# First head ranked in two steps, smaller first loads, and one weight chunk's second use moved behind the first gathers, in a decoder trunk on one core

## The chip, the cores and the metric

The kernel runs on one core of a Trainium2 chip. The metric is the device time of one execution in microseconds (us). The kernel before takes 1578.14 us (median of 3 runs, 1577.06 to 1578.72). Its profiled execution took 1575.86 us, with a span of 1574.0 us from the first to the last instruction.

## The reference

A trunk of two layers over 256 tokens with 1024 features, all in float32. Layer 0 mixes tokens with differential attention, layer 1 with a short gated convolution; behind each comes a product-key expert layer (PEER). Cut to what matters here:

```
def peer_ffn(h, w_q, sub_keys, u_tab, v_tab):
    q = (xt @ w_q).reshape(T, 8, 2, 128)
    s = einsum('thpd,hpkd->thpk', q, sub_keys)          # 2 x 128 scores per head
    s_top, i_top = lax.top_k(s, 16)
    cand = s_top[:, :, 0, :, None] + s_top[:, :, 1, None, :]          # 16 x 16 sums
    cand_idx = i_top[:, :, 0, :, None] * 128 + i_top[:, :, 1, None, :]
    best, pos = lax.top_k(cand, 16); idx = take_along_axis(cand_idx, pos)
    gates = softmax(best)
    act = einsum('chkd,cd->chk', u_tab[idx], x)          # 8 heads x 16 experts per token
    return einsum('chk,chkd->cd', gelu(act) * gates, v_tab[idx])

h = x
for i in range(2):
    h = h + (diff_attention if i == 0 else short_conv)(rmsnorm(h), ...)
    h = h + peer_ffn(rmsnorm(h), ...)
```

Each token picks 128 experts per layer, so the experts' rows (u and v side by side, 2048 floats) are fetched once per token and expert: 512 fetches of 128 rows, 1 MiB each.

## The kernel before

**Windows and slots.** The tokens are two blocks of 128. Window n = 0 and 1 are layer 0 on block 0 and 1, n = 2 and 3 layer 1 on the same blocks. A window's experts are 128 *slots*; slot s fetches one expert row per token. There are 512 slots in all. For each slot GpSimd (POOL) issues an indirect gather into one of the 8 places of `ring` (L643), VectorE (DVE) takes the dot product of the u half with the tokens (`dot`, L1239), ScalarE (ACT) makes gelu, weight and a diagonal matrix (`weigh`, L853 to L859), and TensorE (PE) adds the v half, scaled by that diagonal, into two accumulators (`add_expert`, L575). A gather for slot s waits until slot s-8 has been added (`v_used`). PE runs two slots behind in its own loop: at loop step s it does `add_expert(s-2)` and then the side work that is due at s.

**Weights.** All dense weights come as chunks of 1024 x 512 (2 MiB), issued by SyncE (SP) in the order of the list `loads` into 7 places: two in `wring` (0 and 1), four that lie over pairs of ring places (2 to 5), and `spare` (6). Before a chunk is loaded over another, SP waits in order until PE has finished the chunk that lay there (`written`). `(n, "in", c)` is input chunk c of window n, where c = 0, 1 are Q, 2, 3 are K, and 4, 5 are V; `(n, "out", c)` and `(n, "wq", c)` are the output and query chunks. Window 1's chunks 0, 4 and 5 are not loaded again: PE multiplies them from the places that window 0's copies still hold (`weights`, L297).

**Front.** Before the first slot each engine runs a straight list, `front()`: window 0's attention, its output projection, the query chunk wq 0 in two halves "a" and "b", the ranking of head 0 (`ranked`, L1037: two top-16 searches, the 16 x 16 sums, a top 16 of these, the indices), and window 1's chunks 0, 4 and 5 from places 4, 2 and 3. Since those places are ring places, the gathers of slots 0, 1 (place 4), 4, 5 (place 2) and 6, 7 (place 3) wait for these products (L630 to L638); slots 2 and 3 lie in place 5 and wait for `(0, "out", 0)`.

**Order in the slots.** What comes after is spread over the slots by tables: `AT[1]` for window 1's attention, `LATE_RANK_PROJECT` for wq 1 to 3 of window 0 (product at the slot given, ranking 13 slots later), `LATE_IN_PROJECT` for window 1's remaining input chunks (8 slots of product, then a copy, then on Q and K the norm `norm_qk`). Each of the 8 steps of a chunk's product is one contraction step k, recorded as two matmuls. The next lines are SP's order of loads and the tables:

```
later = [(1, "in", 2), (1, "in", 1), (0, "wq", 2), (1, "in", 3), (0, "wq", 3)]
loads += [(*what, (i + 1) % 2) for i, what in enumerate(later)]
LATE_RANK_PROJECT = {1: 0, 2: 25, 3: 41}
LATE_IN_PROJECT = {2: 9, 1: 17, 3: 33}
```

Of the kernel before, what the change touches and what calls it, by code (L numbers as in the profile page):

```python
# [14 lines left out]
P = 128  # L15
# [41 lines left out]
def steady_of(n):  # L57
# [7 lines left out]
    dict(q0=12, k0=22, q1=30, k1=46,  # L65
         logits0=24, bias0=25, max0=29, exp0=30, diff0=34, turn0=37, values0=40,
         logits1=48, bias1=49, max1=53, exp1=54, diff1=58, turn1=61, values1=64,
         norm0=45, norm1=66, y0=49, y1=70, out0=73, out1=81, h0=82, f0=83, h1=90, f1=91, scale=91,
         wq0=94, wq1=104, wq2=116, wq3=128),
# [54 lines left out]
def build(nc, consts, x_rows, x_cols, bias_rows, ffn_rows, w_qkv, w_o, conv_w_in, conv_w_out, peer_w_q, peer_keys, peer_uv, out):  # L124
    with ExitStack() as ctx:
# [80 lines left out]
        def pool_of(name, banks=None):  # L206
# [6 lines left out]
        x_cols_in = [sem("x_cols_in0"), sem("x_cols_in1")]  # L213
        const_in = sem("const_in")
# [4 lines left out]
        w_half_in = sem("w_half_in")  # L219
# [47 lines left out]
        loads += [(*what, (i + 1) % 2) for i, what in enumerate(later)]  # L267
# [6 lines left out]
        def ring_at(s):  # L274
            return (s + 4) % RING
# [43 lines left out]
        def _(pe):  # L319
# [22 lines left out]
            def project(pool, n, what, c, src, at):  # L342

                for k in range(KT):
                    yield at + k
                    project_part(pool, n, what, c, src, (k,))
# [29 lines left out]
            def mix_values(n, c):  # L376
                copied(pe, tt, *((n, "attn", 2 * c + kb) for kb in range(n + 1)))
                for m in range(n + 1):
                    copied(pe, ff if m else pp, (m, "in", 4 + c))
# [33 lines left out]
            def front():  # L413
# [3 lines left out]
                pe.wait_ge(w_half_in, 16)  # L417
# [3 lines left out]
                for k in every:  # L421
                    if k == 4:
                        pe.wait_ge(x_scaled, 2)
                        pe.wait_ge(w_in[4], 16)
# [58 lines left out]
                project_part(ff, 1, "in", 5, xT1, every)  # L483
# [35 lines left out]
            def output(n):  # L519
                at = steady_of(n)  # L520
                for c in range(2):
                    yield at[f"out{c}"]
                    if c == 0 and n == 1:
                        copied(pe, tt, (1, "y", 0), (1, "y", 1))
# [39 lines left out]
            def add_expert(s):  # L564

                n, k = divmod(s, SLOTS)
                if s == 0:
                    copied(pe, ff, (1, "in", 4), (1, "in", 5))
# [5 lines left out]
                for half in range(2):  # L574
                    mm = nc.tensor.matmul(acc[half][:, :], diag[:, s % RING, :], row[:, D + half * 512:D + (half + 1) * 512],  # L575
                                          start=(k == 0), stop=(k == SLOTS - 1))
                mm.then_inc(v_used, 1)

            front()
            sides = begun(late(1), late_input(2), turn_late("q", 0), late_input(1), turn_late("k", 0), attention(0), late(2),  # L580
                          turn_late("q", 1), late_input(3), late(3), turn_late("k", 1), turn_mixed(0), attention(1), turn_mixed(1),
                          output(1), turn_output(1), *(experts(1, c) for c in range(4)))
# [11 lines left out]
        def _(sp):  # L594
            def load(n, what, c):
                place, landed, _ = weights(n, what, c)
                matrix = {"in": in_dram[n // 2], "out": out_w_dram[n // 2], "wq": peer_w_q[n // 2]}[what]
                if (n, what, c) == (0, "in", 0):
                    half = KT * CHUNK // 2
                    sp.dma_start(place[:, 0:half], matrix[c][:, 0:half]).then_inc(w_half_in, 16)  # L600
                    sp.dma_start(place[:, half:], matrix[c][:, half:]).then_inc(landed, 16)
# [3 lines left out]
            sp.dma_start(xT[:, :, :].rearrange("p k t -> p (k t)"), x_cols[0]).then_inc(x_cols_in[0], 16)  # L605
            previous = {}
            for n, what, c, place in loads:
                if place in previous:
                    m, was, k = previous[place]
                    written(sp, pp, (m, "wqb" if (m, was, k) == (0, "wq", 0) else was, k))  # L610
# [5 lines left out]
            for b in range(2):  # L616
                for c in range(2):
# [6 lines left out]
        def _(pool):  # L624
            for n in range(WINDOWS):
                for k in range(SLOTS):
                    s = n * SLOTS + k
                    if k % TOPK == 0:
                        pool.wait_ge(idx_ready, s // TOPK + 1)
                    if s < RING:  # L630
                        if ring_at(s) < 2:
                            written(pool, ff, (1, "in", 4))
                        elif ring_at(s) < 4:
                            written(pool, ff, (1, "in", 5))
# [665 lines left out]
```

## Time and profile before

| | |
|---|---|
| median of 3 runs | 1578.14 us (1577.06 to 1578.72) |
| profiled execution | 1575.86 us, span 1574.0 us |
| PE, DVE, ACT, POOL busy | 1357.4, 1005.6, 594.8, 568.2 us |
| moved by DMA | 637.58 MB, mean 405 GB/s |
| granted TensorE clock, mean | 0.963 |

The page cuts the span into 40 slices of 39.35 us and gives for each the busy share of the engines and of the DMA engines and the GB/s moved. A busy share averages over stages with different limits, so it is read by stretches: the answers with windows give busy time, instructions, the granted clock, the DMA share and the GB/s of any stretch. The timeline gives single instructions with their start, their length and what ended the idle time before them.

### The profile page before, as it was taken

The page shows a single profiled execution, that of the slowest core. Times are in us where ns is not written, and L with a number is a line of the kernel's source. Part 1 is how long each engine was busy: PE and PEld are TensorE (multiplying, and loading weights), DVE is VectorE, ACT ScalarE, POOL GpSimd, SP SyncE. Part 2 cuts the span into 40 slices and gives each one's busy share as a digit, 9 for nine tenths or more (in the row PEclk, how much of TensorE's full clock was granted, in tenths as well). Part 3 has the DMA queues.
Part 4 walks back from the last instruction along what each step waited for, and adds up shares of the span by engine and source line. Part 5 has one row for each costly group of instructions (what it writes and reads, how often), then busy time and mean ns, then how long its engine had stood idle before and what let it go on. Part 6 is the DMA issues. An engine that isn't in the chain of part 4 may idle for free.

```text
span 1574.0 us, 13058 instructions
## 1 busy us (share of the span) xinstructions
PE 1357.4 (86%) x3288; PEld 587.2 (37%) x3288; DVE 1005.6 (64%) x2442; ACT 594.8 (38%) x1809; POOL 568.2 (36%) x516
## 2 busy tenths in 40 slices
PE   7899899888897988977989898879898887777777
PEld 3454344433343433333434343334343332222222
DVE  5686879964587864444467985444558896544454
ACT  1324354543342542332334443333334444333333
POOL 0024333543343433323444343323344453444341
PEclk9999999999998999989999899999899999999999
DMA  9469999999999999999999999999999999999996
GB/s 399 208 250 422 423 417 407 407 422 421 422 422 421 394 422 423 425 421 422 422 422 422 389 410 423 423 422 422 422 422 421 420 407 421 421 421 422 421 422 282
DMA packets 82297, 637.58 MB, mean 405 GB/s; under 512 B 9136, under 2 KB 9264, under 8 KB 10544
## 3 DMA queue, kind: packets, MB, share of 16 engines
q0 software_dynamic: 73728, 536.90, 82.4%
q1 hardware_dynamic: 7200, 93.85, 14.3%
q10 hardware_dynamic: 1296, 6.00, 0.9%
q8 instruction: 28, 0.46, 0.1%
q14 instruction: 45, 0.37, 0.1%
HBM read 635.67 MB, written 1.05 MB: 405 GB/s over the span
## 4 chain that ended last, share of the span: by engine, by line
DMA 39%; PE 36%; DVE 16%; ACT 4%; issue 4%; DVEq 0%; POOL 0%; SPq 0%; POOLq 0%; ACTq 0%
DMA ring<-in_peer_uv_dram,idx 38%; PE acc L575 22%; PE pp L338 10%; DVE ring L1239 7%; PE acc L338 1%; ACT diag L859 1%; PE tt L351 1%; DVE top_i L1025 1%; ACT weight L855 1%; DVE top L1021 1%; ACT L853 1%; ACT L722 1%; DVE row_f L1070 1%; ACT gelu L853 1%; PE pp L425 1%
## 5 line engine op out<-in xcount | busy, mean ns | idle before, releaser
L575 PE MATMUL acc<-ring,diag 128*128 128x512 f32 x2048 | 1003.9, 618 | 160.4 <-ACT diag L859 150.9
L1239 DVE CUSTOM_DVE_ANT_0 ring<-ring,xf 128x1024 f32<-128x1024 f32 x512 | 626.9, 1226 | 492.2 <-DMA ring<-in_peer_uv_dram,idx 480.5
L643 POOL DMA_INDIRECT ring<-in_peer_uv_dram,idx x512 | 568.0, 1109 | 982.9 <-PE acc L575 856.2
L575 PEld LDWEIGHTS acc<-ring,diag 128*128 128x128 f32 x2048 | 382.8, 196 | 705.3 <-issue 692.8
L853 ACT ACTIVATE gelu<-dots 128x1 f32<-128x1 f32 x512 | 103.5, 202 | 836.7 <-DVE dots L1239 836.4
L859 ACT ACTIVATE diag<-const,weight 128x128 f32<-128x128 f32 x512 | 205.5, 401 | 16.8
L855 ACT ACTIVATE weight<-gelu,gates 128x1 f32<-128x1 f32 x512 | 150.8, 295 | 16.6
L338 PE MATMUL pp<-wring,xT 128*128 128x512 f32 (+1 forms) x272 | 130.5, 578 | 1.2 <-ACT xT L662 1.2
L338 PE MATMUL pp<-wring,rows 128*128 128x512 f32 x192 | 99.6, 600 | 0.0
L338 PEld LDWEIGHTS pp<-wring,xT 128*128 128x128 f32 x272 | 52.0, 194 | 59.4 <-issue 56.5
L338 PE MATMUL pp<-wring,qTa 128*128 128x512 f32 x112 | 57.4, 601 | 0.0
L338 PEld LDWEIGHTS pp<-wring,rows 128*128 128x128 f32 x192 | 36.8, 193 | 45.8 <-issue 45.8
L1239 DVE DVE_READ_ACCUMULATOR2_ANT dots<- 128x1 f32 x512 | 41.9, 82 | 0.0
L410 PE MATMUL ss<-keysT,qT 128*128 128x128 f32 x128 | 21.0, 315 | 20.6 <-issue 20.6
L351 PE MATMUL tt<-const,rows 128*128 128x128 f32 x144 | 23.1, 285 | 17.0 <-DVEq L1199 11.3
L1025 DVE FIND_INDEX8 top_i<-top,score 128x8 uint32<-128x128 f32 x128 | 34.2, 285 | 0.0
L351 PEld LDWEIGHTS tt<-const,rows 128*128 128x128 f32 x144 | 17.7, 146 | 39.8 <-DVEq L1199 14.6
L338 PEld LDWEIGHTS pp<-wring,qTa 128*128 128x128 f32 x112 | 21.7, 195 | 27.2 <-issue 27.2
L410 PEld LDWEIGHTS ss<-keysT,qT 128*128 128x128 f32 x128 | 19.6, 224 | 30.6 <-issue 30.5
L1021 DVE MAX8 top<-score 128x8 f32<-128x128 f32 x128 | 28.1, 280 | 3.4 <-ACT score L718 2.4
L1025 DVE FIND_INDEX8 pos<-best,pick 128x8 uint32<-128x256 f32 x64 | 26.1, 418 | 0.0
L338 PE MATMUL pp<-wring,xf 128*128 128x512 f32 x48 | 25.0, 602 | 0.0
(114 smaller groups left out, 636.5 us busy)
## 6 DMA issues: line engine op xcount, KB each, us to landing
wring<-in_peer_w_q_dram SPq DMA_DIRECT2D x14, 2048.0 KB, 11.9
wring<-in_conv_w_in_dram SPq DMA_DIRECT2D x12, 2048.0 KB, 12.0
wring<-in_w_qkv_dram SPq DMA_DIRECT2D x5, 2048.0 KB, 12.0
ring<-in_peer_uv_dram,idx POOLq DMA_INDIRECT x512, 15.3
wring<-in_conv_w_out_dram SPq DMA_DIRECT2D x4, 2048.0 KB, 11.7
ring<-in_w_qkv_dram SPq DMA_DIRECT2D x3, 2048.0 KB, 32.0
wring<-in_w_o_dram SPq DMA_DIRECT2D x3, 2048.0 KB, 12.6
ring<-in_w_qkv_dram SPq DMA_DIRECT2D x2, 1024.0 KB, 8.6
```

Source lines behind the costliest of these rows:

```text
L338: mm = nc.tensor.matmul(bank[:, 0:width], src[:, k, :], by_row[:, k, columns], start=(k == 0), stop=(k == KT - 1))
L351: t = nc.tensor.transpose(bank[:, j * P:(j + 1) * P], tile, ident)
L410: mm = nc.tensor.matmul(bank[:, j * P:(j + 1) * P], qT[:, j, :], keysT[:, 4 * c + j, :], start=True, stop=True)
L425: mm = nc.tensor.matmul(bank[:, :], xT[:, k, :], by_row[:, k, :], start=(k == 0), stop=(k == KT - 1))
L575: mm = nc.tensor.matmul(acc[half][:, :], diag[:, s % RING, :], row[:, D + half * 512:D + (half + 1) * 512], start=(k == 0), stop=(k == SLO ...
L643: nc.gpsimd.indirect_dma_start(dst, None, uv_dram, bass.IndirectOffsetOnAxis(idx[:, at:at + 1], 0)).then_inc(landed, 16)
L853: nc.scalar.activation(gelu[:, r:r + 1], dots[:, r:r + 1], ACT.Gelu_apprx_tanh).then_inc(gelu_done, 1)
L855: nc.scalar.activation(weight[:, r:r + 1], gelu[:, r:r + 1], ACT.Copy, scale=gates[:, at:at + 1]).then_inc(weight_ready, 1)
L859: nc.scalar.activation(diag[:, r, :], ident, ACT.Copy, scale=weight[:, r:r + 1]).then_inc(diag_ready, 1)
L1021: ins = nc.vector.max(t, v)
L1025: ins = nc.vector.max_index(i, t, v)
L1239: nc.vector.tensor_tensor_reduce(row[:, 0:D], row[:, 0:D], xf[:, s // SLOTS % 2, :], 1.0, 0.0, ALU.mult, ALU.add, dots[:, s % RING:s % RIN ...
```

## The change

Six edits, all but the last in the front and in the first 90 slots.

1. *First loads.* Block 0's columns come in two halves (k 0 to 3, 4 to 7), the first weight chunk in a quarter, a quarter and a half; DVE scales the first half as soon as it is there, PE starts with the first quarter. ACT issues the load of block 0's rows behind the second quarter.
2. *First head.* `first_head` replaces `ranked` for head 0: it finds the best 8 of each half, ranks their 8 x 8 sums, writes 8 indices and releases the gathers of slots 0 to 7; then it does the rest (16 x 16 sums without the 8 found). Block 1's `scale_for_mixer` goes ahead of `add_output`, and the norm of window 1's chunk 0 out of the front into slots 8 to 10.
3. *Chunk (1, "in", 5)* (V of tokens 128 to 255) leaves the front and is multiplied in slots 8 to 15. Chunk (0, "in", 5) therefore lies in `wring` place 0, (0, "in", 1) and (0, "out", 1) in place 3, and both wq 0 and wq 1 in place 1.
4. *Ring.* Slots 0 to 7 now take ring places 6, 7, 2, 3, 4, 5, 0, 1: the first four wait for window 0's output chunks, the next two for (1, "in", 0), the last two for (1, "in", 4).
5. *Tables.* Window 1's other chunks, its attention and window 0's wq 2 and 3 shift by up to 8 slots, and wq 2 is loaded ahead of (1, "in", 1).
6. *End.* The last slot's first half signals by itself; DVE adds it to h while the second half is multiplied, and ACT stores the last quarter of the output.

On SP the chunks from window 0's output on stand so before; in brackets is what the issue waits for, here that PE has finished the chunk that lay there:

```order
L603 DMA ring<-in_w_o_dram 128x4096 [waits pp_written1]
L603 DMA wring<-in_w_o_dram 128x4096 [waits pp_written0]
L603 DMA wring<-in_peer_w_q_dram 128x4096 [waits pp_written1] x2
L603 DMA wring<-in_w_qkv_dram 128x4096 [waits pp_written1]
L603 DMA wring<-in_w_qkv_dram 128x4096 [waits pp_written0]
L603 DMA wring<-in_peer_w_q_dram 128x4096 [waits pp_written1]
```

And so now:

```order
L610 DMA ring<-in_w_o_dram 128x4096 [waits pp_written1]
L610 DMA ring<-in_w_o_dram 128x4096 [waits pp_written0]
L610 DMA wring<-in_peer_w_q_dram 128x4096 [waits pp_written1] x2
L610 DMA wring<-in_w_qkv_dram 128x4096 [waits pp_written1]
L610 DMA wring<-in_peer_w_q_dram 128x4096 [waits pp_written0]
L610 DMA wring<-in_w_qkv_dram 128x4096 [waits pp_written0]
```

The pair of `in_peer_w_q` rows is wq 0 and wq 1. Before, wq 1 waited for (0, "out", 1), now for wq 0's half "b"; the next row, (1, "in", 2), waited for that half "b" and now waits for (1, "in", 5), with wq 2 behind it.

On PE, the end of the front and the first slot before (`acc<-ring,xf` are window 1's chunks from ring places, `uv_in` the landing of a gather):

```order
L338 MATMUL acc<-ring,xf 128x512 [waits ff_read1,w_in2]
L338 MATMUL acc<-ring,xf 128x512 x7
L338 MATMUL acc<-ring,xf 128x512 [waits ff_read0,w_in3]
L338 MATMUL acc<-ring,xf 128x512 x7
L338 MATMUL pp<-wring,xT 128x512 [waits pp_read0,w_in0]
L338 MATMUL pp<-wring,xT 128x512
L575 MATMUL acc<-ring,diag 128x512 [waits uv_in4,diag_ready,ff_read0,ff_read1]
```

And now:

```order
L341 MATMUL acc<-ring,xf 128x512 [waits ff_read1,w_in2]
L341 MATMUL acc<-ring,xf 128x512 x7
L341 MATMUL pp<-wring,xT 128x512 [waits pp_read0,w_in1]
L341 MATMUL pp<-wring,xT 128x512
L581 MATMUL acc<-ring,diag 128x512 [waits uv_in6,diag_ready,ff_read1,ff_read0]
```

The 8 steps of (1, "in", 5) are gone from between (1, "in", 4) and the first slot.

On PE at loop steps 15 to 17 now, where (1, "in", 5) ends and (1, "in", 2) begins:

```order
L341 MATMUL pp<-wring,xf 128x512
L581 MATMUL acc<-ring,diag 128x512 [waits diag_ready,uv_in0]
L581 MATMUL acc<-ring,diag 128x512
L341 MATMUL pp<-wring,xf 128x512 [waits pp_read0,w_in0]
L581 MATMUL acc<-ring,diag 128x512 [waits diag_ready,uv_in1]
```

The row with `w_in0` is the first step of (1, "in", 2); its weights can only be issued once the product in the first row is done.

The diff, cut to its core:

```
-    dict(q0=12, k0=22, q1=30, k1=46,
-         logits0=24, bias0=25, max0=29, exp0=30, diff0=34, turn0=37, values0=40,
...
+    dict(q0=12, k0=29, q1=45, k1=53,
+         logits0=31, bias0=32, max0=36, exp0=37, diff0=41, turn0=44, values0=47,
...
-LATE_RANK_PROJECT = {1: 0, 2: 25, 3: 41}
+LATE_RANK_PROJECT = {1: 0, 2: 24, 3: 48}
-LATE_IN_PROJECT = {2: 9, 1: 17, 3: 33}
+LATE_IN_PROJECT = {5: 8, 2: 16, 1: 32, 3: 40}
+FIRST_NORM = 8
...
-        first = [("in", 0, 4), ("in", 2, 5), ("in", 1, 0), ("in", 3, 1), ("in", 4, 2), ("in", 5, 3), ("out", 0, 5),
-                 ("out", 1, 0), ("wq", 0, 1), ("wq", 1, 0)]
+        first = [("in", 0, 4), ("in", 2, 5), ("in", 1, 3), ("in", 3, 1), ("in", 4, 2), ("in", 5, 0), ("out", 0, 5),
+                 ("out", 1, 3), ("wq", 0, 1), ("wq", 1, 1)]
-        later = [(1, "in", 2), (1, "in", 1), (0, "wq", 2), (1, "in", 3), (0, "wq", 3)]
+        later = [(1, "in", 2), (0, "wq", 2), (1, "in", 1), (1, "in", 3), (0, "wq", 3)]
-        loads += [(*what, (i + 1) % 2) for i, what in enumerate(later)]
+        loads += [(*what, i % 2) for i, what in enumerate(later)]
...
-            return (s + 4) % RING
+            return (6, 7, 2, 3, 4, 5, 0, 1)[s % RING]
...
-                project_part(ff, 1, "in", 5, xT1, every)
...
+            sp.dma_start(xT[:, 0:4, :].rearrange("p k t -> p (k t)"), x_cols[0][:, 0:4 * P]).then_inc(x_first_in, 16)
+            sp.dma_start(first_place[:, 0:CHUNK * 2], in_dram[0][0][:, 0:CHUNK * 2]).then_inc(w_first_in[0], 16)
+            sp.dma_start(xT[:, 4:KT, :].rearrange("p k t -> p (k t)"), x_cols[0][:, 4 * P:]).then_inc(x_cols_in[0], 16)
...
+            def first_head():
+                half = TOPK // 2
+                copied(dve, ss, (0, "scorea", 0))
+                rows2 = [score[:, 0, j, :] for j in range(2)]
+                whole(top8(rows2, [top[:, k, 0:half] for k in range(2)], [top_i[:, k, 0:half] for k in range(2)]))
+                link(nc.vector.tensor_copy(top_f[:, 0:2, 0:half], top_i[:, 0:2, 0:half]))
+                few = pick[:, 48:52, :].rearrange("p a c -> p (a c)")
...
+                whole(top8([few], [best[:, 0, 0:half]], [pos[:, 0, 0:half]]))
+                first_indices(0, half, 3)
+                for j in range(2):
+                    ins = nc.vector.match_replace(rows2[j], top[:, j, 0:half], rows2[j], LOW)
+                link(ins)
...
+                first_indices(half, TOPK, 4)
+                link(nc.vector.tensor_tensor(best_e[:, 0, :], best[:, 0, :], best[:, 0, 0:1].to_broadcast([P, TOPK]), ALU.subtract))
...
-                whole(ranked(0, 0, "a", range(0, 1)))
+                first_head()
                 gate_values(0, 0, range(0, 1))
-                whole(norm_qk(ff, 1, 0))
...
                 for c in range(2):
+                    if n == WINDOWS - 1 and c == 1:
+                        dve.wait_ge(v_used, ALL)
```

## Rows read from the trace of the kernel before

**Rows 1.** The page: GB/s in 40 slices of 39.35 us, and the bytes.

```profile
GB/s 399 208 250 422 423 417 407 407 422 421 422 422 421 394 422 423 425 421 422 422 422 422 389 410 423 423 422 422 422 422 421 420 407 421 421 421 422 421 422 282
DMA packets 82297, 637.58 MB, mean 405 GB/s; under 512 B 9136, under 2 KB 9264, under 8 KB 10544
```

**Rows 2.** Windows: length, busy PE, PEld, DVE, ACT, POOL, clock, DMA share, GB/s.

```profile
58.50:82.40 23.90, 19.16 (x57) 9.30 (x58) 10.22 (x35) 4.55 (x11) 0.00 (x0) 0.93 0.01 2
82.00:112.00 30.00, 28.77 (x95) 16.55 (x95) 25.35 (x93) 5.21 (x13) 6.40 (x6) 1.00 0.67 241
107.00:226.00 119.00, 108.16 (x278) 48.31 (x277) 88.45 (x227) 52.90 (x151) 44.45 (x39) 0.97 1.01 420
226.00:329.00 103.00, 90.25 (x263) 43.30 (x262) 94.37 (x261) 51.57 (x147) 43.27 (x37) 0.95 1.00 408
```

**Rows 3.** Timeline: SP's issues of wq 1 and (1, "in", 2).

```profile
82.41 0.33 SPq L603 DMA_DIRECT2D wring<-in_peer_w_q_dram  x1
93.64 0.33 SPq L603 DMA_DIRECT2D wring<-in_w_qkv_dram  x1
```

**Rows 4.** Timeline: POOL's gathers of slots 0 and 6.

```profile
101.55 1.07 POOL L643 DMA_INDIRECT ring<-in_peer_uv_dram,idx  x1 [101.10 <-DVEq L1078]
113.43 0.94 POOL L643 DMA_INDIRECT ring<-in_peer_uv_dram,idx  x1 [3.96 <-PE acc L338]
```

**Rows 5.** Line L603, SP's weight chunks of 2 MiB: issue to landing.

```profile
DMA to landing us min/median/max: 7.7/12.0/37.7
```

**Rows 6.** Timeline: the first chunks on PE, ACT's next load, the K norm.

```profile
8.81 8.62 PE L425 MATMUL pp<-ring,xT 128*128 128x512 f32 x16 [8.81 <-DMA ring<-in_w_qkv_dram]
16.23 0.34 ACTq L728 DMA_DIRECT2D spare<-in_bias_rows_dram  x1
17.26 7.03 PE L338 MATMUL pp<-ring,xT 128*128 128x512 f32 x16
30.00 0.69 DVE L943 TENSOR_TENSOR rows<-rows,root 128x512 f32<-128x512 f32 x1
30.99 1.04 PE L351 MATMUL tt<-const,rows 128*128 128x128 f32 x8
```

**Rows 7.** Timeline: DVE and ACT around the ranking of head 0.

```profile
78.55 0.69 DVE L1004 TENSOR_TENSOR h<-h,pp 128x512 f32<-128x512 f32 x1 [5.61 <-PE pp L338]
88.35 1.23 DVE L899 CUSTOM_DVE_ANT_0 scratch<-h 128x1024 f32<-128x1024 f32 x1 [0.19 <-DVE xf L1015]
90.19 0.38 ACT L718 ACTIVATE score<-ss 128x256 f32<-128x256 f32 x1 [0.92 <-PE ss L410]
91.83 0.49 DVE L1021 MAX8 top<-score 128x8 f32<-128x128 f32 x2
98.66 0.69 DVE L1064 TENSOR_TENSOR pick<-pos_f,const 128x512 f32<-128x512 f32 x1
102.48 0.69 DVE L904 TENSOR_TENSOR scratch<-rows 128x512 f32<-128x512 f32 x1
107.44 1.23 DVE L1239 CUSTOM_DVE_ANT_0 ring<-ring,xf 128x1024 f32<-128x1024 f32 x1 [0.19 <-DVE rows L943]
```

**Rows 8.** Timeline: PE's additions of slots 0 to 2.

```profile
116.37 1.96 PE L575 MATMUL acc<-ring,diag 128*128 128x512 f32 x4 [1.49 <-ACT diag L859]
119.02 1.88 PE L575 MATMUL acc<-ring,diag 128*128 128x512 f32 x4
121.59 1.88 PE L575 MATMUL acc<-ring,diag 128*128 128x512 f32 x4
```

**Rows 9.** Waits (us, times, longest): PE in 160 to 226 us, DVE in 220 to 230.

```profile
PE acc L575 <- ACT diag L859: 9.1, 4, 3.6
...
DVE ring L1239 <- DMA ring<-in_peer_uv_dram,idx: 5.7, 2, 4.4
```

**Rows 10.** Timeline: the end.

```profile
1570.03 1.52 DVE L1231 TENSOR_TENSOR h<-h,acc 128x512 f32<-128x512 f32 x2 [3.13 <-PE acc L575]
1570.80 1.17 SPq L619 DMA_DIRECT2D out_dram<-h  x2
```

More of the change, by code:

```diff
@@ L345, in project @@
                     yield at + k
+                    if (n, what, c, k) == (1, "out", 0, 4):
+                        copied(pe, tt, (1, "y", 1))
                     project_part(pool, n, what, c, src, (k,))
@@ L576, in add_expert @@
                                           start=(k == 0), stop=(k == SLOTS - 1))
+                    if s == ALL - 1 and half == 0:
+                        mm.then_inc(v_first_used, 1)
                 mm.then_inc(v_used, 1)
             front()
[L580 to L582 removed]
+            sides = begun(late(1), late_input(5), turn_late("q", 0), late_input(2), late(2), turn_late("k", 0), attention(0),
+                          late_input(1), turn_late("q", 1), late_input(3), late(3), turn_late("k", 1), turn_mixed(0), attention(1),
+                          turn_mixed(1), output(1), turn_output(1), *(experts(1, c) for c in range(4)))
             for n in (2, 3):
@@ L616, in _ @@
             for b in range(2):
-                for c in range(2):
+                for c in range(2 - b):
                     sp.wait_ge(h_finished, 2 * (2 + b) + c + 1)
@@ L633, in _ @@
                         elif ring_at(s) < 4:
[L634 removed]
+                            written(pool, pp, (0, "out", 1))
                         elif ring_at(s) < 6:
@@ new lines, in first_indices @@
+            def first_indices(first, last, bits):
+                span = 1 << bits
+                count = last - first
+                where = pos[:, 0, first:last]
+                link(nc.vector.tensor_scalar(pos2[:, 0, 0, 0:count], where, bits, None, ALU.logical_shift_right))
+                link(nc.vector.tensor_scalar(pos2[:, 0, 1, 0:count], where, span - 1, None, ALU.bitwise_and))
+                link(nc.vector.tensor_copy(pos_f[:, 0, :, 0:count], pos2[:, 0, :, 0:count]))
+                shape = [P, 2, count, span]
+                hot = pick[:, 32:48, 0:span].rearrange("p (h k) a -> p h k a", h=2)
+                link(nc.vector.tensor_tensor(hot, pos_f[:, 0, :, 0:count].unsqueeze(3).to_broadcast(shape),
+                                             iota[:, 0:span].unsqueeze(1).unsqueeze(1).to_broadcast(shape), ALU.is_equal))
+                link(nc.vector.tensor_tensor(hot, hot, top_f[:, 0:2, 0:span].unsqueeze(2).to_broadcast(shape), ALU.mult))
+                link(nc.vector.tensor_reduce(row_f[:, 0, :, 0:count], hot, AX.X, ALU.add))
+                link(nc.vector.scalar_tensor_tensor(out=idx_f[:, 0, 0:count], in0=row_f[:, 0, 0, 0:count], scalar=float(NKEYS),
+                                                    in1=row_f[:, 0, 1, 0:count], op0=ALU.mult, op1=ALU.add))
+                link(nc.vector.tensor_copy(idx[:, first:last], idx_f[:, 0, 0:count]))
+                dve.sem_inc(idx_ready, 1)
```

74 lines of the change are left out of this document (52 added, 22 removed).

## The prediction

> **What bounds the kernel now.** I first read the page's GB/s line: outside the first three slices and the last one it stands at 389 to 425, mostly at 421 or 422, and 637.58 MB are moved in all [rows 1]. At 422 GB/s these bytes alone take 1511 us of the span of 1574.0. So the DMA engines are the bound, and no byte goes away: the same 512 gathers, the same chunks. The change can gain only where the DMA engines are idle or underfed, 63 us in all. To find these places I took windows, and grouped them into stretches [rows 2]. From 58.5 to 82.4 us nothing moves (2 GB/s): the chunks of the front have landed and no place is free. From 82 to 112 us it is 241 GB/s, that is 7.23 MB. From 107 to 226 us it is 420, full. From 226 to 329 us it is 408, so 3.4 us are lost against 422 (103 x 14/422), with DVE busy for 94.37 of 103 us. What is lost later lies at the borders of windows, which the change leaves as they are, and at the end.
>
> **How I book.** Where the DMA engines are full before and behind a change, the end shifts by the difference in bytes moved up to a common point, divided by 0.422 MB/us.
>
> **First loads.** PE starts at 8.81 us, when the first half chunk lands, and works 8.62 us, so it could start and end up to 3 us sooner. But the next chunk, (0, "in", 2), is there only at 16.23: ACT's issue at that time had waited for it, and the bytes ahead of it are the same. PE took it up behind its first chunk, at 17.4, and so gains 1.2 us at most [rows 6]. The K norm on DVE hangs on ACT's copies, which come behind that same landing, and still ends at 30.69 (30.00 + 0.69). PE's turns of Q and K ran from 30.99 to 32.03; now the turn of Q runs earlier, that of K from about 30.8 to 31.35. The rest of the front is then 0.7 us earlier. Ends: 0 and 1.2; I take 0.7.
>
> The DMA engines work at 399 GB/s in the first slice already [rows 1]. The Trainium skill, "Perfetto Trace Analysis", section "DMA Optimizations", says that splitting transfers may help if the DMA engines are generally idle, which they are not here. By that rule this term would be 0 and the forecast 0.7 us later; I hold against it that PE waits for one landing, not for all bytes.
>
> **First head.** Block 1's mixer scale (88.35 to 91.7 us, 3.4 us) moves into DVE's idle 5.61 us ahead of the addition at 78.55 [rows 7], which hide it; uncovered it would cost its 3.4. The ranking then starts with the score, which ACT has at 90.6 (90.19 + 0.38), minus 0.7: at 89.9 instead of 91.83. Its steps up to the first 8 indices are shorter forms of rows 7's: two MAX8 (0.49) and two searches for their indices (as long), with gaps 1.2 us; the 64 sums and their best 8 about 0.9; small index steps and casts at 0.17 to 0.2 each, six of them, 1.2; three passes over 128 elements where one over 512 takes 0.69, about 0.8. That is 4.1 us, so the first gather goes at 94.1 instead of 101.55 [rows 4]. The second half takes as long as the rest of the old ranking and a little more, about 6.5 us, the gates 1; at 101.6 the first dot can follow. Before it came at 107.44, behind a norm of 5.0 us (from 102.48) that now lies in slots 8 to 10.
>
> **What the early gathers replace.** Four, then six gathers can be issued from 94.1 to about 101, two more when PE ends (1, "in", 4) at 105.2; before, the last two places came free at 113.43 [rows 4]. But SP pays for it. wq 1 was issued at 82.41, (1, "in", 2) at 93.64 [rows 3]. Now wq 1 waits for what released the latter and goes at 92.9, and (1, "in", 2) only near slot 15. So the idle stretch lasts to 93 and not to 82.4, and a chunk of 2.1 MB, 5.0 us, no longer fills it. From there on the engines are full: wq 1 and six gathers of 1.05 MB are 8.4 MB, 20 us of work, and the next two come after 12. By 112 us: a chunk alone took 7.7 us to land [rows 5] and 5.0 us are its bytes, so 1.6 us go by until the full rate (an estimate), and 17.5 us at 0.42 are 7.36 MB, against 7.23 before. That is 0.13 MB, 0.3 us gained. With the front's shift at 0 or 1.2 instead of 0.7 it runs from 0.4 lost to 0.8 gained. I take 0.3: seven microseconds of earlier indices pay mostly for the chunk that left the gap.
>
> **(1, "in", 5) out of the front.** A chunk's 8 steps take PE 6.9 us (7.03 by the modelled ends [rows 6]), so PE reaches slot 0 at 113.4 - 6.9 - 0.7 = 105.8, and with the same 3 us for ACT's copy and first diagonal the first addition comes at about 109 instead of 116.37. A slot with one step takes PE 2.57 us (119.02 to 121.59) [rows 8]. Loop step 15 ends at 109 + 13 x 2.57 + 1.7, near 144. Until then no chunk is loaded, gathers take 2.48 us each and 4 or 5 are outstanding: full.
>
> **The new wait at slot 16.** At 144 us SP issues (1, "in", 2), and PE asks for it one slot later. Beside gathers a chunk lands in 12.0 us [rows 5], so PE stands for 10 us, to about 156. Behind it wait the additions from slot 15 on, the copies of that chunk on ACT and, through the ring, the gathers from slot 23 on. The cover: outstanding at 144 are 5 gathers, (1, "in", 2) and wq 2, together 9.4 MB or 22 us of DMA work, so the engines do not run dry in these 10 us. At 156 both kernels have added 15 slots, and PE still owes 7 steps of a chunk, 6 us. Before, PE waited for 9.1 us on diagonals between 160 and 226 us [rows 9]; it owes less than it idled. So the wait costs 0, and if this cover fails, up to 6 us.
>
> **Attention and ranking in the slots.** From slot 38 (at 222 us, where DVE last waits for gathers [rows 9]) to slot 75 (329 us) DVE is the bound. The new tables put one more norm (5.0 us) and one more difference (2.5) into slots 39 to 74 and take some 3 us of ranking out: 4.5 us more. But one chunk less has been loaded by slot 38, so this slot comes 5.0 us earlier. Slot 75 then comes at 328.9 - 0.3 - 5.0 + 4.5 = 328.1, which beside the 0.3 is 0.5 us gained. Ends: 3.4 gained (nothing underfed any more) and 4.5 lost (the added work without the earlier start).
>
> **End.** Behind the last matmuls come two additions (1570.03, 1.52 us) and two stores, issued by 1571.97, and the span ends at 1574.0 [rows 10]. Now the first addition runs beside the second half's matmuls (0.94, half of rows 8's 1.88), the second follows them, and the last store is issued about 0.76 us sooner. Ends 0 and 1; I take 0.75.
>
> **Sum.** 0.3 + 0 + 0.5 + 0.75 = 1.55 us. The profiled execution took 1575.86 and would take 1574.3. It lies 2.3 us under the median of the runs shown; taking that as an offset that stays, the forecast is 1578.14 - 1.55 = 1576.6 us. A measurement of this kernel can tell about 0.2%, 3.2 us, from no change, so the forecast is: no measurable change.
>
> **Rivals.**
> - *The underfed stretch fills up* (faster, 0.28). For it: slot 38 comes 5 us earlier, and the first norm falls into slots in which DVE has idle time, since the engines are full and the gathers late there. Against: more of DVE's work than before now lies in slots 39 to 74. Price: 3.4 in place of 0.5, with 0.8 in the front and 0.75 at the end 5 us, 1573.2. It decides from 418 GB/s in the stretch from 226 to 329 us.
> - *The wait at slot 16 is passed on* (slower, 0.16). Place: PE at loop step 16. If the chunk lands late, or PE's idle 9.1 us lay where they can't take up what it owes, 6 us arrive at slot 38 with the DMA engines dry: 1578.1 + 6 - 1.1 = 1583. It decides from a landing more than 22 us behind the issue, or a DMA share under 0.95 between 150 and 226 us.
> - *The early gathers bring their whole lead of 7 us* (0.02): 1570.4, if the engines were idle there anyway. Rows 3 speak against it: wq 1 fills just these microseconds.
>
> **Chances.** Forecast 0.54, with its own range 1574.5 to 1579.5; the two faster cases together 0.30; slower 0.16. For 8 in 10 the range runs from the first rival, 1573.0, to where two thirds of the second are paid, 1581.5. Faster by over 0.2% 0.30, within 0.2% 0.54, slower 0.16.
>
> **What would show it.** First gather near 94, first addition near 109; SP's wq 1 at 93 and nothing moved from 58.5 to 93; a PE wait of 8 to 12 us near 145 with a DMA share of 1.0 beside it; slot 38 near 218 and slot 75 near 328 us; 0.75 us less between the last matmul and the end. Wrong would be: a first gather after 98 us, a DMA share under 0.95 anywhere from 95 to 226 us, or the stretch from 226 to 329 us under 400 or over 418 GB/s.

## The result, and the profile after

The changed kernel takes 1585.65 us (median of 6 runs, 1584.09 to 1588.75), the kernel before on the same chip 1576.69 us (6 runs, 1574.19 to 1578.72): the ratio is 1.0061 with a 95% interval of 1.0046 to 1.0076. It is 9.0 us slower, outside the range given, while the forecast was no measurable change. The profiled execution after took 1588.75 us with a span of 1586.9 us, 12.9 us longer than the span before. It lies 3.1 us above its median and the one before 0.8 us below its own, so the account in bytes below is of this pair of executions (12.9 us) and not of the medians (9.0 us). Of the kernel before on the chip of e9 to e11, one execution of 29 took 1594.18 us at a mean granted clock of 0.847, which widens the intervals of those three runs.

The page of the changed kernel, GB/s in slices (39.67 us each) and the bytes:

```profile
GB/s 396 205 184 423 421 425 313 418 420 423 424 420 422 390 422 424 421 423 424 421 422 423 400 401 424 420 422 422 422 422 421 421 405 421 422 420 422 421 422 297
DMA packets 82586, 637.58 MB, mean 402 GB/s; under 512 B 9169, under 2 KB 9297, under 8 KB 10961
```

The bytes are the same as in [rows 1]. Two slices stand out: the third (184 instead of 250) and the seventh (313 instead of 407). All the others differ by 15 GB/s at most, some up and some down. So there are two places of loss, and they can be priced by bytes. Windows of the changed kernel (length, busy PE, PEld, DVE, ACT, POOL, clock, DMA share, GB/s), against [rows 2]:

```profile
58.50:100.10 41.60, 35.41 (x120) 20.18 (x120) 25.37 (x89) 10.44 (x33) 0.00 (x0) 0.92 0.01 3
82.00:112.00 30.00, 28.77 (x98) 16.60 (x98) 19.95 (x80) 5.66 (x16) 5.92 (x6) 1.00 0.37 144
107.00:226.00 119.00, 107.75 (x281) 49.27 (x280) 84.81 (x221) 46.28 (x130) 39.91 (x39) 0.96 1.01 422
226.00:350.00 124.00, 104.61 (x293) 49.21 (x292) 103.18 (x287) 58.05 (x170) 47.12 (x40) 0.93 0.94 386
260.00:270.00 10.00, 8.23 (x16) 3.97 (x17) 5.36 (x13) 7.71 (x18) 0.93 (x1) 0.66 0.21 82
```

The kernel before in the last two of these windows:

```profile
226.00:350.00 124.00, 111.25 (x312) 52.61 (x311) 106.04 (x279) 59.57 (x173) 55.08 (x46) 0.96 1.00 411
260.00:270.00 10.00, 8.46 (x34) 4.21 (x34) 9.17 (x21) 7.69 (x18) 3.33 (x3) 1.00 1.02 425
```

From 82 to 112 us 4.32 MB were moved instead of 7.23, and 2.91 MB at 0.422 MB/us are **6.9 us**. From 107 to 226 us nothing is lost (422 against 420). From 226 to 350 us it is 25 GB/s less for 124 us, 3.10 MB or **7.3 us**. The end gives 0.8 us back (below). The sum, 13.4 us, stands against 12.9 us of span.

**The first loss starts at 8 us.** Timeline of the changed kernel (start, length, what ended the idle time), against [rows 6]:

```profile
6.22 9.87 PE L432 MATMUL pp<-ring,xT 128*128 128x512 f32 x16 [6.22 <-DMA ring<-in_w_qkv_dram]
8.02 0.34 ACTq L743 DMA_DIRECT2D h<-in_x_rows_dram  x1
18.89 1.23 DVE L917 CUSTOM_DVE_ANT_0 scratch<-h 128x1024 f32<-128x1024 f32 x1 [11.43 <-DMA h<-in_x_rows_dram]
24.06 0.20 ACT L751 ACTIVATE lam_s<-lam_s 128x2 f32<-128x2 f32 x1 [4.11 <-DVEq L944]
24.17 1.25 ACT L672 ACTIVATE rows<-pp,scale_mix 128x512 f32<-128x512 f32 x2
34.24 0.69 DVE L961 TENSOR_TENSOR rows<-rows,root 128x512 f32<-128x512 f32 x1
```

PE does start earlier, 6.22 instead of 8.81. But ACT issues the load of block 0's rows (512 KB) only at 8.02, behind the wait for the second quarter. SP has by then queued its chunks one behind the other, and the rows are in use 10.9 us after their issue. DVE computes the mixer's scale from them and, right behind it, the small sums `lam_sum`. ACT stands for these sums (`DVEq L944`), and its copies need the scale (line L672, `scale_mix`). They begin at 24.17 instead of 19.93, 4.24 us late. DVE's norms of Q and K follow one behind the other, and the K norm ends at 34.93 instead of 30.69 us, again 4.24 late. Before, the load was issued at 1.19 us and DVE read the rows at 9.16:

```profile
1.19 0.45 ACTq L726 DMA_DIRECT2D h<-in_x_rows_dram  x1
9.16 1.22 DVE L899 CUSTOM_DVE_ANT_0 scratch<-h 128x1024 f32<-128x1024 f32 x1 [2.45 <-DMA h<-in_x_rows_dram]
19.93 0.67 ACT L656 ACTIVATE rows<-pp,scale_mix 128x512 f32<-128x512 f32 x1
```

PE, idle for part of that time, shows a granted clock of 0.83 from 30 to 40 us, where before it had 1.00, and 0.83 from 60 to 80 us (0.91 before). 1.00 is 2.4 GHz throughout; 0.83 is a mean of the two levels, 2.4 and 1.2 GHz, over the stretch:

```profile
30.00:40.00 10.00, 7.48 (x21) 3.20 (x19) 8.64 (x33) 1.95 (x3) 0.00 (x0) 0.83 1.00 420
60.00:80.00 20.00, 15.82 (x42) 7.37 (x41) 11.72 (x45) 5.64 (x20) 0.00 (x0) 0.83 0.00 0
```

The score is ready at 97.04 us, 6.5 later than before: 4.24 us are the K norm's, and 2.2 were added on the way. Such an addition also differs between executions with the same front. e3 below has the front of the change, and its K norm ends at 34.74; from 30 to 40 us it shows 1.00, and its score is ready at 95.11, 1.9 us earlier than here. PE's wait ahead is the same in both, 2.52 us for the K norm, but the six matmuls that follow its turn take 4.44 us here and 2.74 in e3. e8 below has the front of the kernel before, with the K norm at 30.73; from 60 to 80 us it shows 0.83, and its score is ready at 92.47, 1.9 us later than before. In order:

```profile
30.00:40.00 10.00, 7.49 (x30) 3.73 (x29) 8.61 (x33) 1.95 (x3) 0.00 (x0) 1.00 1.02 429
60.00:80.00 20.00, 15.99 (x44) 7.96 (x45) 8.91 (x31) 2.69 (x5) 0.00 (x0) 0.83 0.00 0
```

The dip from 30 to 40 us is in two of the four profiled executions with late rows (after and e5, but not e2 and e3) and in none of the nine with early rows; the one from 60 to 80 us comes with either. So about 2 of the 6.5 us came with a clock that a late load didn't bring every time. In bytes: e3 moves 170 GB/s from 82 to 112 us, 5.0 us less than the kernel before, where this execution lacks 6.9. Timeline around the ranking of the changed kernel:

```profile
96.66 0.38 ACT L734 ACTIVATE score<-ss 128x256 f32<-128x256 f32 x1 [0.92 <-PE ss L415]
100.11 0.33 SPq L610 DMA_DIRECT2D wring<-in_peer_w_q_dram  x1
101.12 0.17 DVE L1147 CAST idx<-idx_f 128x8 uint32<-128x8 f32 x1
101.63 1.07 POOL L659 DMA_INDIRECT ring<-in_peer_uv_dram,idx  x1 [101.18 <-DVEq L1148]
```

The shorter ranking works: 4.6 us from score to gather instead of 11.0. It only makes good the delay. The first gather starts as in [rows 4]. But wq 1, issued at 82.41 before [rows 3], goes only at 100.11, and so the DMA engines stand still from 58.5 to 100 us. The chunk that left this gap is missed in full.

**The wait at slot 16 came, and cost nothing.** Changed kernel, SP's next issues and PE:

```profile
153.86 1.88 PE L581 MATMUL acc<-ring,diag 128*128 128x512 f32 x4
154.06 0.33 SPq L610 DMA_DIRECT2D wring<-in_w_qkv_dram  x1
154.43 0.43 SPq L610 DMA_DIRECT2D wring<-in_peer_w_q_dram  x1
165.50 2.07 PE L341 MATMUL pp<-wring,xf 128*128 128x512 f32 x2 [9.76 <-DMA wring<-in_w_qkv_dram]
```

PE stood for 9.76 us, from 155.7 to 165.5, while the engines moved 426 GB/s.

**The second loss is in slots 41 to 50.** Timeline of DVE, PE and POOL there:

```profile
243.67 1.22 DVE L1314 CUSTOM_DVE_ANT_0 ring<-ring,xf 128x1024 f32<-128x1024 f32 x1
251.04 1.22 DVE L1314 CUSTOM_DVE_ANT_0 ring<-ring,xf 128x1024 f32<-128x1024 f32 x1
253.41 3.05 PE L581 MATMUL acc<-ring,diag 128*128 128x512 f32 x4 [4.12 <-ACT diag L875]
255.58 1.23 DVE L1314 CUSTOM_DVE_ANT_0 ring<-ring,xf 128x1024 f32<-128x1024 f32 x1 [0.18 <-DVE rows L961]
256.25 1.06 PE L356 MATMUL tt<-const,scratch 128*128 128x128 f32 x4
261.77 1.09 PE L356 MATMUL tt<-const,rows 128*128 128x128 f32 x4 [4.46 <-ACT scratch L672]
268.22 0.93 POOL L659 DMA_INDIRECT ring<-in_peer_uv_dram,idx  x1 [10.56 <-PE acc L581]
```

Three consecutive dots (slots 42 to 44) are 7.4 and 4.5 us apart, where the engines' pace is one gather in 2.48 us. Between them DVE works off the ranking of wq 2, the norm of (1, "in", 1) and the attention's difference, which the new tables place in the same slots. PE waits 4.12 us for a diagonal. Then it waits a second time, at loop step 45. The pool `tt` has two banks. The turns of the attention at steps 44 and 45 hold both, and the turn of Q (`q1=45`) needs the first of them back; ACT frees it only behind the `weigh` of slot 45, which itself waits for that slot's dot. This costs 4.46 us more. POOL, held by `v_used`, stands for 7.53 us ahead of its gather at 256.73 and for 10.56 us ahead of the one at 268.22, and between 260 and 270 us the DMA engines run at a share of 0.21, 82 GB/s.

**The end.** Changed kernel, against [rows 10]:

```profile
1581.73 1.96 PE L581 MATMUL acc<-ring,diag 128*128 128x512 f32 x4 [0.52 <-ACT diag L875]
1582.86 0.69 DVE L1306 TENSOR_TENSOR h<-h,acc 128x512 f32<-128x512 f32 x1 [2.28 <-PE acc L581]
1583.64 0.33 SPq L631 DMA_DIRECT2D out_dram<-h  x1
1583.72 0.69 DVE L1306 TENSOR_TENSOR h<-h,acc 128x512 f32<-128x512 f32 x1 [0.17 <-PE acc L581]
1584.50 0.35 ACTq L887 DMA_DIRECT2D out_dram<-h  x1
```

From the start of the last four matmuls to the end of the span it is 5.2 us (1581.73 to 1586.9); before it was 6.0 us:

```profile
1568.04 1.96 PE L575 MATMUL acc<-ring,diag 128*128 128x512 f32 x4 [0.52 <-ACT diag L859]
```

### The profile page after: what moved, and what is told of

The parts are those of the page before. It is cut to its first block, busy times and chain, and to the rows that moved or that the text cites. A ratio compares the mean times of both kernels' runs of the same rounds, so it can differ in the third digit from the quotient of the medians.

```text
span 1586.9 us, 13075 instructions
## 1 busy us (share of the span) xinstructions
PE 1363.1 (86%) x3288; PEld 587.2 (37%) x3288; DVE 1006.1 (63%) x2452; ACT 595.2 (38%) x1809; POOL 563.6 (36%) x516
## 4 chain that ended last, share of the span: by engine, by line
DMA 42%; PE 36%; DVE 14%; issue 4%; ACT 4%; POOL 0%; DVEq 0%; SPq 0%; POOLq 0%; ACTq 0%
DMA ring<-in_peer_uv_dram,idx 40%; PE acc L581 23%; PE pp L341 10%; DVE ring L1314 6%; PE tt L356 1%; PE acc L341 1%; ACT diag L875 1%; ACT weight L871 1%; DMA wring<-in_w_qkv_dram 1%; DVE top_i L1043 1%; DMA h<-in_x_rows_dram 1%; DVE top L1039 1%; PE ss L415 1%; ACT gelu L869 1%; DVE pick L1085 1%
## 5 line engine op out<-in xcount | busy, mean ns | idle before, releaser
L341 PE MATMUL pp<-wring,qTa 128*128 128x512 f32 x96 | 49.0, 592 | 0.0
L341 PE MATMUL pp<-wring,xf 128*128 128x512 f32 x64 | 34.8, 626 | 9.8 <-DMA wring<-in_w_qkv_dram 9.8
L1043 DVE FIND_INDEX8 top_i<-top,score 128x8 uint32<-128x128 f32 x128 | 34.2, 285 | 0.0
L415 PE MATMUL ss<-keysT,qT 128*128 128x128 f32 x128 | 19.3, 297 | 13.4 <-issue 13.4
L341 PEld LDWEIGHTS pp<-wring,qTa 128*128 128x128 f32 x96 | 18.5, 193 | 23.2 <-issue 23.2
L1043 DVE FIND_INDEX8 pos<-best,pick 128x8 uint32<-128x256 f32 (+1 forms) x64 | 25.8, 415 | 0.0
```

The lines of the kernel that those rows point to most:

```text
L341: mm = nc.tensor.matmul(bank[:, 0:width], src[:, k, :], by_row[:, k, columns], start=(k == 0), stop=(k == KT - 1))
L415: mm = nc.tensor.matmul(bank[:, j * P:(j + 1) * P], qT[:, j, :], keysT[:, 4 * c + j, :], start=True, stop=True)
L1043: ins = nc.vector.max_index(i, t, v)
```

## The experiments

The theory after the result: loss A comes from the late issue of block 0's rows, loss B from what the tables stack in slots 41 to 50. The rivals: A comes from the four split transfers or from the displaced wq 1, and B follows from A or from the wait at slot 16. Each ratio is to the kernel before on the same chip. The unaltered change did not run beside e1 to e4.

**e1: the rows issued at once.** The change, without ACT's wait:

```
-                act.wait_ge(w_first_in[1], 16)
                 act.dma_start(h[:, 0, :], x_rows[0]).then_inc(x_in[0], 16)
```

> The changed kernel, but block 0's rows are loaded right behind the constants, as before the change. Theory H (the late load of these rows delays DVE's first statistics, ACT's first copy and with it the whole front): rows land near 9 us, first gather near 94 to 95 us instead of 101.6, and the end is 6 to 8 us earlier than the changed kernel's, 1578 to 1580 us. Rival (the front is held by PE or by the first chunks, the rows' load only lies beside it): first gather still after 100 us, time within 2 us of the changed kernel's 1585.7.

Measured: 1582.34 us, ratio 1.0043 [1.003, 1.0057]. Windows of e1:

```profile
82.00:112.00 30.00, 27.28 (x92) 15.63 (x91) 22.20 (x85) 9.04 (x24) 7.88 (x8) 1.00 0.55 222
226.00:350.00 124.00, 103.97 (x294) 49.25 (x294) 102.05 (x270) 57.29 (x164) 44.86 (x40) 0.93 0.95 390
```

The first gather goes at 96.11 us and the front moves 222 GB/s instead of 144, which is 5.5 us by bytes. The median of e1 falls by 3.3 us against the change's first runs and by 5.6 against its later ones (e5), less than the 6 to 8 expected. Counted over the kernel before on each chip it is 2.4 and 5.0 us, and the interval overlaps that of the change, so the time of e1 alone is a weak witness; the bytes and e4 carry the finding. Loss B stays (390 GB/s), so it does not follow from A.

**e2: the rows issued late, in the kernel before.** The counter-test:

```
+                act.wait_ge(w_half_in, 16)
                 act.dma_start(h[:, 0, :], x_rows[0]).then_inc(x_in[0], 16)
```

> The kernel before, but ACT waits for the first half weight chunk before it issues the load of block 0's rows. Theory H: rows land near 19 us instead of 9, first gather 5 to 8 us later than 101.6, time 5 to 8 us over the kernel before (1582 to 1585 us). Rival (the late load alone costs nothing; it costs only with the other edits of the front): same as before within 1.5 us.

Measured: 1581.0 us, ratio 1.0029 [1.002, 1.0038], 5.3 us over the kernel before, at the low end of the 5 to 8 expected. Timeline of e2:

```profile
7.29 0.34 ACTq L727 DMA_DIRECT2D h<-in_x_rows_dram  x1
18.12 1.23 DVE L900 CUSTOM_DVE_ANT_0 scratch<-h 128x1024 f32<-128x1024 f32 x1 [11.68 <-DMA h<-in_x_rows_dram]
105.89 1.08 POOL L643 DMA_INDIRECT ring<-in_peer_uv_dram,idx  x1 [105.44 <-DVEq L1079]
```

One wait on one load, with nothing else of the change, gives the same landing (10.8 us), the K norm at 34.2 (33.47 + 0.69, not shown) and 4.3 us on the first gather. From 82 to 112 us e2 moves 188 GB/s instead of 241, 3.8 us by bytes. Loss A is shown from both sides: taking the wait out moves the front forward, and putting it in alone moves it back.

**e3: the second Q turn out of step 45.** The change with

```
-    dict(q0=12, k0=29, q1=45, k1=53,
+    dict(q0=12, k0=29, q1=48, k1=53,
```

> The changed kernel with one number of the table altered: PE turns window 1's second Q chunk at slot 48 instead of 45, where two turns of the attention weights already stand. Theory T (three turns at one loop step need a bank that ACT frees only behind a later slot's dot product, so PE stops for it and the gathers dry up): no PE wait on the copy of the attention weights near 260 us, the 10 us with 82 GB/s go, 3 to 6 us faster than the changed kernel. Rival D (DVE has three jobs stacked in slots 41 to 43, and that alone starves the ring): PE waits for diagonals instead, under 1.5 us gained.

Measured: 1583.0 us, ratio 1.0047 [1.0033, 1.0061]; the wait on `ACT scratch` is gone. Windows of e3:

```profile
226.00:350.00 124.00, 108.03 (x305) 50.69 (x304) 106.41 (x285) 61.70 (x178) 45.02 (x41) 0.96 0.99 405
260.00:270.00 10.00, 7.22 (x33) 4.20 (x32) 6.48 (x12) 7.96 (x19) 1.88 (x2) 1.00 0.81 279
```

405 instead of 386 GB/s is 5.6 us by bytes; the median is 2.7 to 5.0 us lower (1.7 and 4.4 counted over the kernel before on each chip; this interval too overlaps that of the change). So by bytes most of loss B hung on one turn that asked for a bank still held.

**e4: both mended** (e1 and e3 together).

> The changed kernel with both edits: block 0's rows loaded early, second Q turn at slot 48. If the two losses are separate places in the ledger of bytes, the gains add: 9 to 14 us under the changed kernel, 1572 to 1577 us. If the second loss only takes up room that the first one left (or the reverse), the sum is smaller by several microseconds.

Measured: 1578.59 us, ratio 1.0018 [1.0009, 1.0027]. Windows of e4:

```profile
82.00:112.00 30.00, 27.28 (x92) 15.61 (x91) 23.30 (x91) 9.08 (x23) 8.02 (x9) 1.00 0.60 240
226.00:350.00 124.00, 108.68 (x306) 51.12 (x307) 105.45 (x273) 60.36 (x173) 43.87 (x41) 0.96 0.99 405
```

First gather at 94.79, wq 1 at 93.28, 7.20 MB from 82 to 112 us, first addition at 109.14: the front of the prediction (94.1, 92.9, 7.36 MB, 109), once the rows come in time. e1 has the same front and moved 222 GB/s there where e4 moved 240; the 1.3 us between them is what single executions differ by. The two repairs together give 7.1 us against the change's first runs and 9.4 against e5, where the single ones add up to 6.0 and 10.6. The interval is clear of that of the change. wq 1 is displaced in e4 as in the change, so this rival for loss A is out. The 1572 to 1577 us expected were missed by 1.6 us. What is left is 405 against 411 GB/s; e6 asks whether that is DVE's stack.

**e5: the change once more**, on the chip of e6 to e8.

> The changed kernel once more, unaltered, beside the next ones on the same chip: about 1585 us and 9 us over the kernel before. First gather between 99 and 102 us. If it comes out under 1583, part of the 3.3 and 2.7 us read from the two single edits was between chips and not theirs.

Measured: 1587.99 us, ratio 1.0066 [1.0052, 1.008]. The result stands.

**e6: the attention's steps apart.** e4, and the difference, its turns and its values three slots later, the value norm and its turn two slots later, the Q turn ahead of them:

```
-    dict(q0=12, k0=29, q1=48, k1=53,
-         ... diff0=41, turn0=44, values0=47, ... norm0=52, ... y0=56, ...
+    dict(q0=12, k0=29, q1=46, k1=53,
+         ... diff0=44, turn0=47, values0=50, ... norm0=54, ... y0=58, ...
```

> The changed kernel with early row load, and window 1's first attention half pulled apart on DVE: difference, turns and values 3 slots later (44, 47, 50), its value norm at 54, the second Q turn at slot 46 ahead of the turns. Theory D2 (what is left of the loss in the stretch from 226 to 350 us is DVE's stack of ranking, norm and difference in slots 41 to 43): no DVE slot over 6 us there, the stretch at 410 GB/s or more where e4 had 405, 1 to 2 us under e4's 1578.6. Rival (the stretch is bound by DVE's total work, so spreading it does nothing): 405 GB/s and e4's time within 0.8 us.

Measured: 1575.59 us, ratio 0.9994 [0.9985, 1.0003]. Windows of e6:

```profile
82.00:112.00 30.00, 27.28 (x91) 15.56 (x90) 23.25 (x91) 9.09 (x23) 8.19 (x9) 1.00 0.60 242
226.00:350.00 124.00, 110.42 (x313) 51.86 (x314) 107.16 (x276) 61.08 (x177) 48.75 (x42) 0.97 1.01 417
```

Same work, no less of it on DVE (107.16 us busy, more than in any other of these windows), and yet 417 GB/s. It was not the amount but the place. It is 3.0 us quicker than e4 on another chip, with intervals that don't overlap, more than the 1 to 2 expected; the bytes say 3.5. The wait at slot 16 is still in it, so loss B doesn't come from there. With all three repairs the change is what was forecast, no measurable difference.

**e7: the first head alone.** The kernel before, with `first_head` in place of `ranked`, the two scales moved ahead, and a ring order in which four early gathers find a place:

```
-            return (s + 4) % RING
+            return (6, 7, 4, 5, 0, 1, 2, 3)[s % RING]
...
-                whole(ranked(0, 0, "a", range(0, 1)))
+                first_head()
```

> The kernel before with the two-step ranking of head 0, block 1's mixer scale moved ahead, and the ring order 6, 7, 4, 5, 0, 1, 2, 3, but with all weight chunks, products, first loads and tables as before. Ledger theory (early gathers pay in full when the weight chunks keep their place in the gap): first gather near 95 us, the DMA engines busy from 95 us on without the hole near 101 us, about 9.2 MB moved from 82 to 112 us instead of 7.2, 3 to 5 us faster than before. Rival (DVE's later stretch takes the gain back): under 1 us gained.

Measured: 1575.1 us, ratio 0.9989 [0.998, 0.9998]. Windows of e7:

```profile
82.00:112.00 30.00, 28.77 (x96) 16.48 (x95) 24.10 (x96) 5.22 (x13) 6.81 (x6) 1.00 0.79 309
112.00:226.00 114.00, 104.94 (x277) 47.78 (x276) 85.80 (x223) 54.79 (x155) 41.08 (x38) 0.97 1.01 411
```

Here wq 1 and (1, "in", 2) stay in the gap and the early gathers come on top: 9.27 MB by 112 us against 7.23, worth 4.8 us. But from 112 to 226 us 11 GB/s less are moved, which takes 3.0 us back. The net is 1.2 us in the medians, less than the 3 to 5 expected. The trace shows where the second stretch falls off, in its first 20 us (423 GB/s before), and what the next gather waits for:

```profile
112.00:132.00 20.00, 18.51 (x44) 7.94 (x43) 16.56 (x43) 12.53 (x33) 8.25 (x8) 1.00 0.98 358
118.81 0.94 POOL L647 DMA_INDIRECT ring<-in_peer_uv_dram,idx  x1 [3.41 <-PE acc L575]
```

The ring has 8 places, so the ninth gather waits for the first addition. That addition comes at 116.08 against 116.37 before, since the additions still stand behind the same products of the front, and the ninth gather goes at 118.81 against 118.59. So the eight gathers use up their lead, and no further gather can follow earlier than before. No run tests this by itself, but e9 and e11 show the same dip (362 and 359 GB/s).

**e8: the end alone.** The kernel before with only edit 6.

> The kernel before with only the split of the last slot and its stores. 0.75 us less between the last matmul and the end; in the time 0.3 to 1 us less, hardly to be told from nothing.

Measured: 1575.25 us, ratio 0.9997 [0.9988, 1.0006]: no difference that the runs can tell. In the profile of e8 it is 5.1 us from the last matmuls (1570.26) to the end of the span (1575.4), 0.8 less than before.

**e9: first head and end.** e7 with the new end.

> The kernel before with two parts of the change: the first head in two steps (with its ring order and the block 1 scale moved ahead) and the new end. Each alone measured 0.9989 and 0.9997 of the kernel before. Theory (the changed parts are additive, both are small gains): the profile shows about 0.8 us less from the last matmul to the end (5.1 to 5.2 instead of 5.96), a first gather at 94 to 96, and a time 1.0 to 2.5 us under the kernel before, ratio 0.9984 to 0.9993. Rival (the first head's gain lies inside what executions differ by, and only the end is real): 0.9993 to 1.0000.

Measured: 1573.15 us, ratio 0.9976 [0.9955, 0.9996], 3.3 us under the kernel before on that chip (1576.46), more than the 1.0 to 2.5 expected.

**e10: the split loads alone**, in the kernel before, the rows issued at once:

```
+            sp.dma_start(xT[:, 0:4, :] ..., x_cols[0][:, 0:4 * P]).then_inc(x_first_in, 16)
+            sp.dma_start(first_place[:, 0:CHUNK * 2], ...).then_inc(w_first_in[0], 16)
+            sp.dma_start(xT[:, 4:KT, :] ..., x_cols[0][:, 4 * P:]).then_inc(x_cols_in[0], 16)
```

> The kernel before with the first loads split as in the change (columns in halves, first chunk in a quarter, a quarter and a half), but ACT issues block 0's rows at once, as before. Theory A (the split is harmless, the loss of the change sits in the late issue of the rows alone): DVE reads the rows at 9 to 10 us, the K norm ends within 1.5 us of 30.7, ratio 0.9990 to 1.0005, first gather 100 to 102.5. Theory B (four transfers beside the rows slow the rows down, so the split itself costs): rows land at 12 us or later, K norm past 32, first gather past 103, ratio 1.001 to 1.003. The prediction's own term was 0.7 us earlier.

Measured: 1575.96 us, ratio 0.9991 [0.997, 1.0011]. DVE reads the rows at 8.70 us and the first gather goes at 101.06, 0.5 earlier than before. The K norm ends at 30.95. The split is harmless, and the rival that it slows the rows down is out. Whether the split gains its half microsecond the time can't tell.

**e11: first head, end and split together.**

> First head in two steps, new end and the split first loads with block 0's rows issued at once: every part of the change except the moved V chunk and the tables. Theory (the parts add up): ratio 0.9980 to 0.9993, the quickest of all; against the change with its three faults mended (0.9994) it says what the moved chunk is worth: if this one is 0.5 to 2 us quicker, moving the chunk out of the front was itself a small loss. Rival (the moved chunk gains as much as it costs): within 0.5 us of that one, ratio 0.9990 to 0.9998.

Measured: 1573.14 us, ratio 0.997 [0.995, 0.9989]. It is level with e9, so the split adds nothing that can be told. Both are 3.3 us, 0.2%, under the median of the kernel before, with intervals that end just under 1.

Against e6 (1575.59), which has every part and the moved chunk, e11 is 2.5 us quicker. They ran on different chips and the intervals overlap, so this is not a measured difference. The bytes point the same way for e6 and e9: by 112 us 242 against 309 GB/s, 2.0 MB or 4.8 us for e9, and from 112 to 226 us 422 against 412, 2.7 us back.

## Why the prediction was wrong, step by step

- **First loads: the step that failed first.** It was booked as 0.7 us earlier, bounds 0 and 1.2. It priced SP's three transfers and PE's start, and took the K norm as hanging "on ACT's copies, which come behind that same landing". It left out that the copies also need the scale and the sums that DVE makes behind the landing of block 0's rows, and that the diff puts this load behind a wait. The row that showed the need was within reach: DVE read the rows at 9.16 us, 2.45 us after it had become idle. Moved by 6.8 us (1.19 to 8.02) and landing 2.9 us more slowly, the load came at 18.89 and set the K norm 4.24 us late. A bound of the loss, "the load lands in 8 us again", would have given 16 us and thereby a warning. The range went from 0 to 1.2 gained. In place of that the front as a whole lost 6.9 us by bytes in the profiled execution (5.0 in e3); about 2 us of this are the clock's, and differ between executions of one front. e1 and e2 show the cause. With the rows in time the term was nearly right: the first gather of e10 is 0.5 us earlier, against 0.7 taken.
- **First head.** Right in itself: 4.1 us to the indices were forecast, and 4.3 measured (97.04 to 101.29, the end of the last cast). The lead of 7 us was eaten by the step above. In e4 it is there, with the first gather at 94.79.
- **What the early gathers replace.** Right in e4: 7.20 MB against 7.36 forecast and 7.23 before. The seven microseconds pay for the displaced wq 1, as argued. e7 shows the other side: with wq 1 left in the gap 9.27 MB get through. The rival "they bring their whole lead" fell by the same displacement. The working had one slip: 7.7 us less the 5.0 of the bytes are 2.7 us and not 1.6, which would have given 6.9 MB and 0.8 us lost; the measured 7.20 MB lie between.
- **(1, "in", 5) out of the front.** Forecast was a first addition near 109; it came at 115.97, 0.4 us earlier than [rows 8] and not 7, by the delay of the front. In e4, without that delay, it comes at 109.14, as forecast.
- **The wait at slot 16.** Forecast 10 us of PE, at no cost; measured 9.76 us at 426 GB/s. It began at 155.7 instead of near 145. The forecast of "slower" was hung on this wait being passed on, with a price of 6 us. The kernel did become slower, but not by this rival. Its sign of recognition, a DMA share under 0.95 between 150 and 226 us, did not occur. The sign is blunt, though: in e7 the share stood at 0.98 in a stretch with 358 GB/s, so GB/s is the column to read.
- **Attention and ranking: the step that failed second.** It was booked as 0.5 us gained, ends 3.4 gained and 4.5 lost; 7.3 us were lost by bytes up to 350 us (379 instead of 408 GB/s from 226 to 329). The working added up DVE's work over 36 slots and set it against a start that is earlier. The sum was not the matter: e6 has the same work and 417 GB/s. What failed is the step from a total to a time: three pieces fall into the same three slots (e6 takes them apart and gains 12 GB/s over e4), and the turn of Q at step 45 finds both banks held (e3 moves it and gains 19). The bound of 4.5 us, all added work paid, was no bound, since a wait of PE for a bank was not in it.
- **End.** 0.75 forecast, 0.8 in the profiles of the change and of e8. It is under what the runs can tell alone.
- **The signs named** did their work: a first gather after 98 us, and under 400 GB/s from 226 to 329 us, were both given as what would prove the forecast wrong, and both occurred (101.63 us, 379 GB/s).

What stays open: a run that tests the reading of the dip behind 112 us in e7, e9 and e11, and what exactly separates the 3.3 and 5.6 us of e1's repair. The unaltered change gave 1585.65 and 1587.99 us on two occasions, and its single executions had spans between 1582.3 and 1586.9. How much of that spread is the clock can't be told from the profiled executions alone.

## What to carry to other kernels

Read a diff of loads for what it does to the transfers it does not mention: a small load moved behind a wait lands behind all that was queued meanwhile, and everything computed from it has to be followed up to the first product. When work is moved in a table of slots, lay out what each engine has in each slot of the new table, and for each turn which banks earlier turns still hold: a total over a stretch hides three pieces in neighbouring slots. And before a faster engine is credited, see which transfer filled the time that it frees.

## What the runs showed of the chip

- The 512 KB rows took 10.8 to 10.9 us from issue to use when issued at 7.3 to 8.0 us on ACT's queue, behind chunks that SP had queued before, in two kernels (8.02 to 18.89, 7.29 to 18.12). Issued at 1.19 us they were in use at 9.16.
- With PE idle for part of 20 to 40 us the change's granted clock was 0.83 over 30 to 40 us in two executions (after, e5) and 1.00 in a third with the same front (e3); the score came at 97.04 and 96.88 us against 95.11. Behind the waits in slots 43 to 45 it was 0.66 over 260 to 270 us. So two executions of one front can lie 1.9 us apart at the score. None of the nine profiled executions with early rows fell under 1.00 in that stretch.
- PE could stand for 9.8 us without loss just when two chunks (4.2 MB, 10 us at 422 GB/s) had been issued beside the gathers; in slots 41 to 50, waits of 7.53 and 10.56 us ahead of two gathers took the DMA share to 0.21 from 260 to 270 us.
